# Head sums in two rounded passes, one visit of the solve dissolved, and the second chunk mirrored, in a one-core hybrid attention and RWKV-7 layer

## What is computed

```python
kk = kk / jnp.maximum(jnp.sqrt(jnp.sum(kk * kk, axis=-1, keepdims=True)), 1e-12)   # "kn"
S = S * w_t[:, :, None, :] + sa[..., None] * (kk_t * a_t)[:, :, None, :] + v_t[..., None] * k_t[:, :, None, :]
mean = jnp.mean(o, axis=-1, keepdims=True)                                           # "mean"
var = jnp.mean(jnp.square(o - mean), axis=-1, keepdims=True)                         # "var"
bonus = jnp.sum(rh * kh * r_k, axis=-1, keepdims=True) * vh                          # "bo"
```

## Time and profile before

| | |
|---|---|
| median of three runs | 3245.78 us |
| profiled execution, its own time | 3246.72 us |
| span of it, first to last instruction | 3244.7 us |
| TensorE busy | 3171.4 us (98%) |
| VectorE busy | 1625.4 us (50%) |
| ScalarE busy | 1022.0 us (31%) |
| GpSimd busy | 232.5 us (7%) |
| mean granted clock of TensorE | 0.997 |

### The profile page before, as it was taken

How to read it: one execution, slowest core, us unless ns; L and a number is a source line. 1 busy time by engine, 2 the same in 40 slices (tenths; PEclk the granted TensorE clock), 3 DMA queues, 4 the chain that set the end, 5 groups by cost and what they waited for, 6 DMA issues and landing times.

```text
span 3244.7 us, 65733 instructions
## 1 busy us (share of the span) xinstructions
PE 3171.4 (98%) x27835; PEld 2663.8 (82%) x27835; DVE 1625.4 (50%) x2742; ACT 1022.0 (31%) x1858; POOL 232.5 (7%) x229
## 2 busy tenths in 40 slices
PE   8999999999999999999999999999999999999998
PEld 6777778877777878877777878998777789999997
DVE  6566554567766573454553256304555525432224
ACT  5444333344443443232222034302333312310001
POOL 0021100011011000111110000001111100000000
PEclk9999999999999999999999999999999999999999
DMA  4454443376666753554444673265343445465556
GB/s 160 155 190 161 147 154 97 104 233 203 196 215 215 254 188 97 163 157 144 138 143 146 193 237 102 92 210 167 125 124 125 134 158 168 147 192 181 176 176 196
DMA packets 269442, 532.27 MB, mean 164 GB/s; under 512 B 34016, under 2 KB 37728, under 8 KB 269152
## 3 DMA queue, kind: packets, MB, share of 16 engines
q1 hardware_dynamic: 269152, 528.07, 50.6%
HBM read 415.97 MB, written 112.08 MB: 163 GB/s over the span
## 4 chain that ended last, share of the span: by engine, by line
PE 89%; DVE 6%; DMA 2%; ACT 1%; issue 1%; SPq 0%; POOL 0%; DVEq 0%; ACTq 0%; POOLq 0%
PE PS L824 76%; PE PS L863 6%; PE PS L921 1%; PE PS L976 1%; DMA y<-xres 1%; DMA wl<-weight_lo 1%; DMA raw<-w 1%; DVE wl L1585 1%; PE PS L997 1%; PE PS L1147 1%; DVE op L2077 1%; PE PS L911 0%; PE PS L1161 0%; PE PS L1165 0%; ACT L1176 0%
## 5 line engine op out<-in xcount | busy, mean ns | idle before, releaser
L824 PE MATMUL PS<-hh,wh 128*128 128x512 f32 x1864 | 766.2, 411 | 0.9 <-ACT gst L1235 0.9
L824 PE MATMUL PS<-hh,wl 128*128 128x512 f32 x1864 | 728.9, 391 | 0.0
L824 PE MATMUL PS<-hl,wh 128*128 128x512 f32 x1864 | 727.9, 391 | 0.0
L1195 ACT ACTIVATE wh<-raw 128x512 fp32r<-128x512 f32 x452 | 284.1, 630 | 481.2 <-PE PS L824 365.7
L824 PEld LDWEIGHTS PS<-hh,wh 128*128 128x128 f32 x1864 | 350.3, 188 | 91.2 <-issue 14.3
L1585 DVE TENSOR_TENSOR wl<-raw,wh 128x512 fp32r<-128x512 f32 x452 | 321.6, 714 | 194.4 <-ACT wh L1195 189.2
L824 PEld LDWEIGHTS PS<-hh,wl 128*128 128x128 f32 x1864 | 350.4, 188 | 76.0
L824 PEld LDWEIGHTS PS<-hl,wh 128*128 128x128 f32 x1864 | 351.1, 188 | 73.7 <-issue 8.1
L824 PE MATMUL PS<-hh_last,wh 128*128 128x272 f32 x1280 | 266.1, 289 | 2.0 <-DVE xres L1717 2.0
L824 PE MATMUL PS<-hl_last,wh 128*128 128x272 f32 x1280 | 264.6, 288 | 0.0
L824 PE MATMUL PS<-hh_last,wl 128*128 128x272 f32 x1280 | 263.2, 287 | 0.0
(11 more groups left out here) (284 smaller groups left out, 4815.7 us busy)
## 6 DMA issues: line engine op xcount, KB each, us to landing
wh<-weight_hi SPq DMA_DIRECT2D x500, 256.0 KB, 2.7
wl<-weight_lo SPq DMA_DIRECT2D x500, 256.0 KB, 3.0
raw<-w SPq DMA_DIRECT2D x186, 512.0 KB, 3.6
weight_hi<-wh SPq DMA_DIRECT2D x164, 256.0 KB, 4.4
weight_lo<-wl SPq DMA_DIRECT2D x164, 256.0 KB, 4.7
raw<-w SPq DMA_DIRECT2D x76, 256.0 KB, 3.4
gate_scratch<-gst SPq DMA_DIRECT2D x48, 256.0 KB, 3.8
gb<-gate_scratch SPq DMA_DIRECT2D x24, 512.0 KB, 5.1
```

What stands on the lines that cost most here:

```text
L824: mm = pe.matmul(PS[:, bank(t) + f, 0:t.cols], wt[:, cols], mov[:, m, (t.half + f) * t.cols:(t.half + f + 1) * t.cols], start=(first and a ...
L1195: act.activation(wh[h % 4][:], src, ACT.Copy).then_inc(hi_done, 1)
```

## The change

The four head sums are split as the product is. ScalarE writes a rounded copy (`ksh`, `bh`, `mh`, `vh`), VectorE the remainder (`ksl`, `bl`, `ml`, `vl`), and `head_sum` runs two float32r matmuls with a rounded head matrix. The square before `var` is now VectorE's (`sq`), beside ScalarE's rounded square.

```diff
+            def head_sum(bank_, n, hi, lo):
+                pe.matmul(PS[:, bank_, 0:n], head[:], hi[...], start=True, stop=False)
+                return pe.matmul(PS[:, bank_, 0:n], head[:], lo[...], start=False, stop=True)
...
                 yield pr.t("KG")
-                pe.wait_ge(V, pr.at("V", f"sub{pr.chs[-1]}"))
+                pe.wait_ge(V, pr.at("V", "ksl"))
-                pe.matmul(PS[:, 4, 0:4 * W], mat[:, M_HEAD], flat(pp), start=True, stop=True).then_inc(Tn, 1)
+                head_sum(4, 4 * W, cch, ktl).then_inc(Tn, 1)
...
                 yield pr.t("BO")
-                pe.wait_ge(G, pr.at("G", "bo2"))
+                pe.wait_ge(V, pr.at("V", "bl"))
-                pe.matmul(PS[:, 3, 0:4 * W], mat[:, M_HEAD], flat(cc), start=True, stop=True).then_inc(Tn, 1)
+                head_sum(4, 4 * W, pph, ccl).then_inc(Tn, 1)
...
                 yield pr.t("MEAN")
-                pe.wait_ge(V2, pr.at("V2", f"oO{pr.chs[-1]}"))
+                pe.wait_ge(V2, pr.at("V2", "ml"))
+                head_sum(b0_, 4 * W, oph, yol).then_inc(T2, 1)
                 yield pr.t("VAR")
-                pe.wait_ge(A2, pr.at("A2", "osq"))
+                pe.wait_ge(V2, pr.at("V2", "vl"))
+                head_sum(b1_, 4 * W, yol, ool).then_inc(T2, 1)
```

On VectorE, `ksl` has the tag ZA 0.2, `bl` the tag PV 0.9 (behind `atl`), `ml` stands behind `oO1`, `st11` and `st21` of DO1, and `sq` and `vl` stand behind `oc` at MEAN 0.25:

```diff
+                yield pr.t("PV", 0.9)
+                dve.wait_ge(A, pr.at("A", "bh"))
+                tt_("bl", fl_(ccl), fl_(cc), fl_(pph), ALU.subtract)
...
+                dve.wait_ge(A2, pr.at("A2", "mh"))
+                tt_("ml", fl_(yol), fl_(oo), fl_(oph), ALU.subtract)
                 yield pr.t("MEAN", 0.25)
...
+                own("oc")
+                tt_("sq", fl_(oo), fl_(op), fl_(op), ALU.mult)
+                dve.wait_ge(A2, pr.at("A2", "vh"))
+                own("sq")
+                tt_("vl", fl_(ool), fl_(oo), fl_(yol), ALU.subtract)
```

Visit XT goes. Its products for `xd` move behind those of PV, `xv` behind those of S4, the transposes `tok0` behind S6 and `tok1` behind S7; the product `lv` moves from S5 to S8, and the copies follow. The weights are set anew:

```diff
-... ("BO", 3.0), ("LM", 4.0), ("XT", 3.5),
-         ("S1", 2.0), ("S2", 2.5), ("S3", 2.0), ("S4", 1.5), ...
+... ("BO", 3.0), ("LM", 5.0),
+         ("S1", 2.2), ("S2", 2.5), ("S3", 2.0), ("S4", 1.8), ...
```

The operations on `lm` are reordered (`lmO`, `yd`, then `lmE`). Chunk 1's solve uses the halves opposite to those it used, so that S1 becomes:

```diff
                 yield pr.t("S1")
-                for c in pr.chs:
-                    pe.wait_ge(V, pr.at("V", f"xd{c}"))
-                    pe.wait_ge(A, pr.at("A", f"tok{c}"))
-                    for j in range(4):
-                        tiles(c, home, home, 5 + 2 * c, 0, of(yd[c]), of(xd[c]), j)
+                pe.wait_ge(V, pr.at("V", f"ydO{pr.chs[-1]}"))
+                for j in range(4):
+                    for c in pr.chs:
+                        tiles(c, home, own, 5 + 2 * c, 0, of(yd[c]), of(xd[c]), j)
```

More of the change, by code:

```diff
@@ L241, in steps @@
         s = by("mx") + ["mx2"] + by("sub") + ["msk"] * (first or sample) + ["sk"]
-        s += ["n1", "zp"] + ["lwm"] * sample + ["scan", "sum", "den", "rec", "pn", "kt1", "kt2"] + ["ktm"] * sample
+        s += ["ksl", "n1", "zp"] + ["lwm"] * sample + ["scan", "sum", "den", "rec", "pn", "kt1", "kt2"] + ["ktm"] * sample
         s += ["bb"] + ["bbm"] * sample
-        s += ["at", "rt", "pc", "btE", "btO", "ktE", "ktO", "atl", "bv"]
-        s += each("lmE", "lmO", "ydE", "ydO") + each("xd", "svE", "svO")
+        s += ["at", "rt", "pc", "btE", "btO", "ktE", "ktO", "atl", "bl", "xd0"] + ["xd1"] * (not sample) + ["bv"]
+        s += each("lmO", "ydE", "ydO") + ["pt1E1", "pt1O1"] * (not sample) + each("lmE")
+        s += ["yoE1", "yoO1"] * (not sample)
         for n in ("pt2", "pt3", "dt", "rr", "tt"):
             s += [f"{n}0"] + ([] if sample else [f"{n}E1", f"{n}O1"])
+            if n == "dt":
+                s += each("svE", "svO")
         return s
     if engine == "V2":
-        s = ["x0", "saE0", "saO0"] + (["st10", "st20", "oE0", "oO0", "x1", "saE1", "saO1"] if not sample else [])
+        s = ["x0", "saE0", "saO0"] + (["st10", "st20", "oE0", "oO0", "xE1", "xO1", "saE1", "saO1"] if not sample else [])
         c = chs[-1]
-        return s + [f"oE{c}", f"oO{c}", f"st1{c}", f"st2{c}", "oc", "on", "lg", "ob", "gate"]
+        return s + [f"oE{c}", f"oO{c}", f"st1{c}", f"st2{c}", "ml", "oc", "sq", "vl", "on", "lg", "ob", "gate"]
     if engine == "A":
-        s = ["ksq", "vt", "z0", "z1", "z2", "z3", "a0", "a1", "a2", "a3", "ex", "es", "n2", "n3", "pm", "p", "ip"]
-        return s + by("ptr") + ["ath"] + by("tok", "xy2", "xy4", "x8", "d", "zl", "g", "h") + ["gc"]
+        s = ["ksq", "vt", "ksh", "z0", "z1", "z2", "z3", "a0", "a1", "a2", "a3", "ex", "es", "n2", "n3", "pm", "p", "ip"]
+        return s + by("ptr") + ["bh", "ath"] + by("xy2", "xy4", "x8", "d", "g") + ["tok0"] + by("h") + ["tok1"] * (not sample) + by("zl") + ["gc"]
     if engine == "A2":
-        return each("o1") + ["osq", "v1", "v2", "rwh"]
+        return each("o1") + ["mh", "vh", "v1", "v2", "rwh"]
     if engine == "G":
-        return ["kk", "cm", "kkn", "bo1", "bo2"] + by("pt1") + each("yoE", "yoO") + ["lb"]
+        return ["kk", "cm", "kkn", "bo1", "bo2", "pt10", "yoE0", "yoO0", "lb"]
     if engine == "G2":
@@ L441, in hybrid_layer @@
         hw0, ha0, hka = (new(n, [128, 4]) for n in ("hw0", "ha0", "hka"))
-        mat = new("mat", [128, M_MEAN, 128])
+        mat = new("mat", [128, M_HEAD, 128])
+        head = new("head", [128, 128], F32R)
         lora = new("lora", [128, 2, 512])
@@ L857, in norms2 @@
                         norm_sum(b, accn, 7).then_inc(n2_ms, 1)
+            def head_sum(bank_, n, hi, lo):
+                pe.matmul(PS[:, bank_, 0:n], head[:], hi[:].rearrange("p a w -> p (a w)")[:, 0:n], start=True, stop=False)
+                return pe.matmul(PS[:, bank_, 0:n], head[:], lo[:].rearrange("p a w -> p (a w)")[:, 0:n], start=False, stop=True)
             def tiles(c, src, dst, bank_, col_, lhs, rhs, j):
@@ L1047, in front @@
                     for c in pr.chs:
-                        mm = tiles(c, home, own, 4 + 2 * c, 0, of(xd[c]), of(pts[c][2]), j)
+                        mm = tiles(c, own, home, 4 + 2 * c, 0, of(xd[c]), of(pts[c][2]), j)
                         if j == 3:
                             step(f"s4_{c}")
+                            mm.then_inc(Tn, 1)
+                for j in range(4):
+                    for c in pr.chs:
+                        mm = tiles(c, own, away, 3 + 2 * c, 0, lambda r, j, par: xsl(8 + j, r, CH * c, CH * c + CH),
+                                   lambda r, j, par: mat[r, M_ID, r], j)
+                        if j == 3:
+                            step(f"xv{c}")
                             mm.then_inc(Tn, 1)
@@ L1056, in front @@
                     for c in pr.chs:
-                        mm = tiles(c, own, home, 5 + 2 * c, 0, of(pts[c][3]), lambda r, j, par: mat[r, M_ID, r], j)
+                        mm = tiles(c, home, own, 4 + 2 * c, 0, of(pts[c][3]), lambda r, j, par: mat[r, M_ID, r], j)
                         if j == 3:
                             step(f"s5_{c}")
[L1060 to L1066, removed]
                             mm.then_inc(Tn, 1)
@@ L1099, in front @@
                     for c in pr.chs:
-                        mm = tiles(c, home, own, 4 + 2 * c, 0, of(xd[c]), of(pts[c][4]), j)
+                        mm = tiles(c, own, home, 4 + 2 * c, 0, of(xd[c]), of(pts[c][4]), j)
                         if j == 3:
@@ L1103, in front @@
                             mm.then_inc(Tn, 1)
+                for j in range(4):
+                    for c in pr.chs:
+                        mm = tiles(c, away, own, 5 + 2 * c, 0, lambda r, j, par: lm[c][r, par, j, CH:128],
+                                   lambda r, j, par: sv[c][r, j, par, :], j)
+                        if j == 3:
+                            step(f"lv{c}")
+                            mm.then_inc(Tn, 1)
+                pe.wait_ge(A, pr.at("A", f"tok{pr.chs[-1]}"))
                 pe.wait_ge(gp1, b + 1)
                 for j in range(4):
-                    mm = low_rank(5, slice(0, 128), 1, 13, j)
+                    mm = low_rank(3, slice(0, 128), 1, 13, j)
                 step("g")
@@ L1129, in tail @@
                     pe.wait_ge(V, pr.at("V", "tt" + last(pr.chs[-1])))
+                    pe.wait_ge(A, pr.at("A", f"zl{pr.chs[-1]}"))
                     for j in range(4):
-                        first = tiles(c, own, own, b1_, 0, lambda r, j, par: ra[r, j * n + c, 1, :], of(st), j)
-                        mm = tiles(c, own, other, b0_, 0, of(st), lambda r, j, par: ra[r, j * n + c, 0, :], j)
+                        first = tiles(c, own, home, b1_, 0, lambda r, j, par: ra[r, j * n + c, 1, :], of(st), j)
+                        mm = tiles(c, own, away, b0_, 0, of(st), lambda r, j, par: ra[r, j * n + c, 0, :], j)
                     step(f"q0{c}")
@@ L1305, in norm1 @@
                     act.wait_ge(n1_ms, u + 1)
+                    if b == 0:
+                        act.wait_ge(ld, LDALL)
+                        act.activation(head[:], q[:, 0, 0:128], ACT.Copy).then_inc(head_in, 1)
                     log_table()
@@ L1415, in front @@
```

(28 more changed lines are left out.)

181 lines of the change are left out of this document (106 added, 75 removed).

## The result

The changed kernel takes 3281.03 us, the median of four runs (3278.38 to 3285.0), against 3244.82 us before: a ratio of 1.0113 with a 95% interval of 1.0097 to 1.0129. It is slower by 36 us. The direction is the one forecast; the size is four times what was forecast, and 2 us beyond the upper end of the range. Two single runs further down, 6223 us in `e7` and 6416 us in `f3`, took about twice as long as the other runs of their kernels and are left out of the medians.

What follows compares the result with a forecast made beforehand. PE, busy 98% of the span, was taken to bound the kernel: 3246.7 - 46 - 4 + 37 + 12 + 5 + 5 = 3255.7, less 0.9 against the runs' median, about 3254 us; range 3222 to 3279.

Steps and rivals of the forecast that it cites:

- PE's work: On PE: shorter head sums -26.8, S1 -14.8, dissolved visit XT -6.1, PV's shape change +1.7; together 46 us less.
- S1: Visit S1 alternates over four quadrants instead of two and falls from 2.22 to 1.3 us, -14.8 us in all.
- PV's new products: In PV, 64 x 64 products follow 128-row ones; the shape change costs 0.1 us a pair, bounds 0 and 0.37, +1.7 in all.
- 37 at BO: PE's new waits at BO for `bl`, queued late on VectorE: +37 us, lower end about 23, upper 45.
- 12 at MEAN: PE's new waits at MEAN for `ml`, behind ScalarE's copy and two state operations: +12 us, between 6 and 15.
- 5 around: Waits around MEAN: 1 or 2 us at VAR in the first batch, +3 at DO1 from split `x1`; together +5, bounds 0 and 10.
- -4 eased: Two waits of PE ease: LM's for `bv` (2.9 us) and about 1 us at S5; together -4 us.
- The clock: Half clock on PE behind long new waits, mostly BO's: three falls taken, +5 us, bounds 0 and 12.
- my list of `atl`'s lateness: For all 17 pairs, how far `atl` on VectorE ends behind BO's start before the change, -2.1 to 5.8 us; positives sum to 40.
- my own row: Profile row before the change: behind PE's 2.2 us wait at DO1 the clock was at 0.50 for 3.4 us, costing 1.7 us.
- The rival in which VectorE falls behind: VectorE also late in the first batch: BO 45, MEAN 16, others 12, clock 10, so 3279 us; chance 0.15.
- Only the fixed chain counts: BO waits only 23 us, the chain from `var`, MEAN 6, rest 2, no clock falls: 3227 us; chance 0.26.

Runs made afterwards that it cites:

- e7: On top of e2, S1's products issued chunk 0 first and then chunk 1, as before the change, on the mirrored halves; 3227.3 us, ratio 0.9949.
- f3: The changed kernel with only the sums at KG and VAR split, those at BO and MEAN in one float32 pass, against the kernel before; 3214.86 us, ratio 0.9904.
- e2: The changed kernel with nothing taken out, `bl` moved on VectorE from PV 0.9 to PV 0.1, ahead of the tail's operations; 3216.03 us, ratio 0.9913.
- e3: The changed kernel with 0 to 21 unread matmuls per pair on PE ahead of the wait at BO; 3259.85 us, ratio 1.0047.

## Why the prediction was wrong

**PE's work: right in kind, 4 us too much.** Forecast -46 us, found -41.7; in `e2`, with the same work and without BO's waits, the same account gives -43.4. The head sum measured 0.47 instead of 0.45, S1 was right to 0.01 us, and PV's new products cost 0.17 us beyond their own time where I had taken 0.1. This is its timeline:

```profile
784.96 0.39 PE L834 MATMUL PS<-fh,wl 128*128 128x512 f32 x1
785.18 0.40 PE L871 MATMUL PS<-yol,head 128*128 128x512 f32 x1
785.42 0.39 PE L872 MATMUL PS<-ool,head 128*128 128x512 f32 x1
785.74 1.08 PE L972 MATMUL PS<-ptk,both_lm 128*64 128x256 f32 x8
786.75 0.69 PE L878 MATMUL PS<-bkk,ra 64*64 64x64 f32 x32
787.38 0.50 PE L834 MATMUL PS<-fh,wh 128*128 128x512 f32 x1
787.71 0.39 PE L834 MATMUL PS<-fl,wh 128*128 128x512 f32 x1
```

787.71 - 784.96 - 0.45 = 2.30, against 0.45 for the sum, 1.21 for PV's own products with the fixed part (from the same pair before: 777.69 - 775.17 - 0.45 - 0.86), and 0.47 for the new 32 records; 0.17 is left. By the Trainium skill ("TensorEngine Tiling (Array Packing)", Key Properties) a change of tiling mode drains TensorE; here that is no more than 0.17 us, under half of what a whole visit's fixed part costs, and the dissolved visit still pays.

**The waits together: right, by luck; each one not.** Forecast +50 us (37 at BO, 12 at MEAN, 5 around, -4 eased), found +52.3: BO was 8 us longer, MEAN 5 shorter, the eased wait gave 2.9 and the rest 2.9 more. BO alone was 45.2, at the upper bound. It waits 15 times, and the largest miss was the pair of the earlier trace rows, where I had 0.1 us and PE waited 4. On VectorE in front of this `bl`, between `ktO` and `atl`, now stands a product operation of 1.80 us in place of 0.69:

```profile
793.25 0.69 DVE L1929 TENSOR_TENSOR bkk<-kt__110,ip__109 64x512 f32<-64x512 f32 x1
793.97 1.80 DVE L1626 TENSOR_TENSOR wl<-raw,wh 128x512 fp32r<-128x512 f32 x1
795.70 0.68 DVE L1929 TENSOR_TENSOR atl<-PS,ath 128x512 fp32r<-128x512 f32 x1
796.30 0.68 DVE L1929 TENSOR_TENSOR ccl<-cc__107,pph 128x512 fp32r<-128x512 f32 x1
```

GpSimd's `rwl` runs beside it, from 793.96 to 795.22. Such an operation stands there in three pairs; in seven more it is `bl` itself that meets `rwl` and takes 1.19 us where I had 0.69 (in two others 1.03 and 1.46), as in the third pair:

```profile
310.92 1.27 POOL L1613 TENSOR_TENSOR rwl<-op,rwh 128x512 fp32r<-128x512 f32 x1 [12.44 <-ACT rwh L1504]
310.93 0.69 DVE L1929 TENSOR_TENSOR atl<-PS,ath 128x512 fp32r<-128x512 f32 x1
311.54 1.19 DVE L1929 TENSOR_TENSOR ccl<-cc__107,pph 128x512 fp32r<-128x512 f32 x1
```

I had priced the lateness down as accidental. It was not: `rwl` follows `gate` as `bl` does, so that `bl` or an operation ahead of it meets `rwl` in most of the pairs. `atl` starts with `rwl` too and still takes 0.69; one of its inputs lies in PSUM. That this is the reason isn't shown.

MEAN went the other way: 10.1 us where 3.0 stood, so 7 and not 12. The line before:

```profile
PE PS L1161 <- DVE oo L2077: 3.0, 3, 1.1
```

I had read 12 from tails that already waited, where the state operations end last; in the others ScalarE's copy and they were done in time.

**The clock: wrong, and the step that failed.** I wrote "I take three falls, +5 (bounds 0 and 12)", beside the remark that six or seven of BO's waits were longer than the one that had been followed by a fall. Found were eleven falls at BO in place of three, three of them of two stretches: 14 stretches more than before and +22.1 us. `e3` shows that they come from the waits: it gave back 21 us with the time of the wait left in. Eleven of the 15 waits at BO, of 2.2 to 5.2 us, had half clock behind them; those of 0.4, 2.0 and 2.1 us and the last pair's of 2.8 had not. The mechanism was named and had a row; the number of falls was halved without a reason, and each was priced at one stretch. Even the count of long waits was low: my list of `atl`'s lateness, with its 0.32 added, has nine above 2.2 us, and twelve were found. With the waits as forecast and the price of my own row, 7 x 1.7 = 12 us give 3261 us and nine give 3264; the rest of the clock's price comes from waits that were more, or longer, than I had them.

Term by term, the profiled span ended 24 us above the forecast: 17 of them are the clock, 8 BO and 4 PE's work, and MEAN's 5 went the other way (the small ones together gave 1 back). The rival in which VectorE falls behind comes out at 3279, but by another sum: it gave 45 to BO, 10 to the clock, 16 to MEAN, and 12 to waits at S2, S6 and elsewhere that aren't there.

**The rival on the other side.** "Only the fixed chain counts" gave 3227 with BO at 23 us. It is false for this kernel. Yet the chain it priced was the lever: `bl` needs nothing of `on` to `atl`, and taken out from behind them, no wait for it is left.

## What to carry to other kernels

When a wait is added to the engine that bounds the kernel, look at what stands in front of the awaited operation in its engine's list, not only at what it depends on. A remainder that is ready early but queued late costs as much as one that is computed late. And price a wait of TensorE twice: a second time for the half clock that the trace shows behind waits of that length, for each of them. As a forecast that is near the upper side: here eleven of the twelve waits at BO of 2.2 us and more had it, while other waits of 2.7 and 3.0 us in the same kernel hadn't.

## What the runs showed of the hardware

- At eleven waits at BO the product ran at half clock for 3.4 us or twice that, at four it did not. Length doesn't settle it: one of 2.0 us before the change was followed by half clock (at 1945.8) and one of 3.0 (up to 145.4) was not, and the wait for `rwh` of 3.0 us was in `e2` and not in the changed kernel. Matmuls that nobody reads, put into the wait, kept the clock up and made the kernel 21 us faster.
- A 128 x 512 subtraction on VectorE took 1.80 us instead of 0.69 while GpSimd ran its `rwl` on tiles of the same size (793.97 to 795.77 beside 793.96 to 795.22). One such product operation stood ahead of `bl` in three of the pairs, and `bl` itself took 1.19 us in seven. `atl`, which reads PSUM, took 0.69 beside it.
- Products of 64 x 64 on four quadrants in turn take half the time of those on two. Where two chunks use different pairs of quadrants one after the other, they overlap at the seam: 2.04 us in place of 2.22.
